# GLA: where VectorE computes the running gate sums and the low parts; mLSTM: where TensorE waits for the meta rows

## The reference, cut to what matters

```python
g = log_sigmoid(a_lr @ w_gla_a2 + b_gla_a) / GLA_TAU      # a log decay for each key feature
def gla_chunk_step(S, xs):
    q, k, v, g = xs
    G = cumsum(g, axis=2)                                  # the running gate sums
    decay = exp(where(causal, G[t] - G[s], -inf))
    A = einsum("bhtk,bhtsk,bhsk->bhts", q, decay, k)
    o = (q * exp(G)) @ S + A @ v
...
o = rms_norm(o, g_gla_head) * silu(r)
y_a = o @ w_br_gla
# mLSTM: q, k (through a convolution), v, and two gates are further columns of the same projection
```

## Time and profile before

| | us |
|---|---|
| median of three executions | 1351.56 |
| lowest and highest of them | 1349.48 and 1355.84 |
| the profiled execution, its own time | 1352.61 |
| its span, first to last instruction | 1350.9 |
| TensorE busy in it | 1294.3 (96%) |
| VectorE busy in it | 622.4 (46%) |
| mean granted TensorE clock | 0.989 of full |

### The profile page before, as it was taken

One profiled execution on the slowest core, in us unless ns is written; L12 is line 12 of the kernel. 1 busy time (PEld: TensorE's weight loads), 2 busy tenths in 40 slices (PEclk: granted clock), 3 DMA queues, 4 the chain that ended last, 5 costly groups with the idle time before them and its releaser, 6 DMA issues.

```text
span 1350.9 us, 17177 instructions
## 1 busy us (share of the span) xinstructions
PE 1294.3 (96%) x6445; PEld 1040.0 (77%) x6448; DVE 622.4 (46%) x1114; ACT 386.8 (29%) x787; POOL 778.0 (58%) x918
## 2 busy tenths in 40 slices
PE   6999889999999999999989999999899999999997
PEld 4866777766898777777888897788678888888886
DVE  3245797773246757462255554232621111333334
ACT  4243334544003333223113344130611111222322
POOL 8367331042663644455765555587467777888882
PEclk9999999999999999999999999999989999999999
DMA  7963200042322212212334332252233333222221
GB/s 179 222 224 90 77 16 16 22 121 60 94 68 61 63 48 63 57 53 64 100 94 112 94 94 81 69 187 94 58 90 94 95 94 115 88 96 96 96 80 63
DMA packets 168441, 121.10 MB, mean 90 GB/s; under 512 B 12264, under 2 KB 146510, under 8 KB 168358
## 3 DMA queue, kind: packets, MB, share of 16 engines
q1 hardware_dynamic: 161654, 108.84, 28.3%
q10 hardware_dynamic: 6704, 11.15, 2.6%
HBM read 115.72 MB, written 9.62 MB: 93 GB/s over the span
## 4 chain that ended last, share of the span: by engine, by line
PE 83%; DVE 9%; DMA 2%; issue 2%; SPq 2%; ACT 1%; POOL 1%; DVEq 0%; ACTq 0%; POOLq 0%
PE GP L1723 40%; PE PA L1758 8%; PE GP L1758 7%; PE GP L1738 6%; PE GP L1720 5%; PE GP L1924 2%; PE PA L1881 2%; DMA wraw<-in_w_in 2%; PE PA L2061 2%; PE PA L1973 1%; PE PA L1904 1%; DVE S L1229 1%; PE PA L1960 1%; DVE top L1228 1%; DVE hres L1648 1%
## 5 line engine op out<-in xcount | busy, mean ns | idle before, releaser
L605 POOL TENSOR_TENSOR wlo<-wraw,whi 128x256 fp32r<-128x256 f32 x712 | 576.6, 840 | 14.9
L601 POOL TENSOR_SCALAR whi<-wraw 128x1024 fp32r<-128x1024 f32 x178 | 194.2, 1091 | 531.0 <-PE GP L1723 261.3
L1723 PE MATMUL GP<-xh,whi 128*128 128x512 f32 x368 | 154.7, 420 | 3.9 <-POOL wlo L605 1.6
L1723 PE MATMUL GP<-xl,whi 128*128 128x512 f32 x368 | 147.4, 400 | 0.0
L1723 PE MATMUL GP<-xh,wlo 128*128 128x512 f32 x368 | 147.1, 400 | 0.0
L1676 DVE TENSOR_TENSOR ul<-U,uh 128x512 fp32r<-128x512 f32 x64 | 65.5, 1060 | 106.6 <-ACT uh L1110 106.6
L1723 PE MATMUL GP<-nh,whi 128*128 128x512 f32 x256 | 102.6, 401 | 0.7 <-DVE nl L1660 0.7
L1723 PE MATMUL GP<-nl,whi 128*128 128x512 f32 x256 | 102.4, 400 | 0.0
L1723 PE MATMUL GP<-nh,wlo 128*128 128x512 f32 x256 | 102.4, 400 | 0.0
L1680 DVE TENSOR_TENSOR U<-U 128x512 f32<-128x512 f32 x32 | 34.5, 1079 | 145.7 <-ACT U L1114 145.7
L1723 PEld LDWEIGHTS GP<-xh,whi 128*128 128x128 f32 x368 | 70.9, 193 | 22.9 <-issue 4.5
(11 more groups left out here) (373 smaller groups left out, 2705.2 us busy)
## 6 DMA issues: line engine op xcount, KB each, us to landing
wraw<-in_w_in SPq DMA_DIRECT2D x75, 512.0 KB, 3.8
wraw<-in_w_up SPq DMA_DIRECT2D x32, 512.0 KB, 4.0
wraw<-in_w_down SPq DMA_DIRECT2D x32, 512.0 KB, 3.6
line_rows<-bias_line SPq DMA_DIRECT2D x1, 5240.0 KB, 26.4
table<-line_rows SPq DMA_DIRECT2D x1, 4096.0 KB, 14.7
wraw<-in_w_br_dsa SPq DMA_DIRECT2D x8, 512.0 KB, 4.1
wraw<-in_w_br_gla SPq DMA_DIRECT2D x8, 512.0 KB, 4.1
wraw<-in_w_br_ml SPq DMA_DIRECT2D x8, 512.0 KB, 4.0
```

What stands on the lines that cost most here:

```text
L601: nc.gpsimd.tensor_scalar(hi, src, 1.0, 1.0, ALU.mult, ALU.mult).then_inc(hi_done, 1)
L605: part = nc.gpsimd.tensor_tensor(lo[:, at:to], src[:, at:to], hi[:, at:to].bitcast(FP32), ALU.subtract)
L1723: ins = mm(ps[0:t.m, 0:SEQ], wt[:, s0, w], av, start=st, stop=sp_)
```

## The change

It has three parts. The function `forget` is cut in two: its PSUM read stays where it was, and the rest becomes `forget_sums`, which VectorE now runs at the off-diagonals, after the second scaling (q = 1); head 0's own is called right after `forget(0)`. `low_parts(0, h - 1)` moves to the off-diagonals too, after the first scaling (q = 0). On TensorE the wait for `xt_ok` moves from ahead of `mq0` to ahead of `mv0M`. No instruction is added or removed, and neither ScalarE's nor GpSimd's order changes.

```diff
--- before.py
+++ after.py
@@ -1336,6 +1336,10 @@
                 g0 = G[:, h % 2, :]
                 dve.wait_ge(gg_l, h + 1)
                 ts(two(g0), halves(ps), cc("a2", h), 0.0, ALU.add, ALU.min).then_inc(gfree[tl[f"gg{h}"].slot], 1)
+
+            def forget_sums(h):
+
+                g0 = G[:, h % 2, :]
                 whole(f"gg{h}")
                 seq(tt(gch[:, :], g0, gch[:, :], ALU.subtract))
                 nc.vector.tensor_tensor_scan(g0[:, 0:META], ones[:, 0:META], gch[:, 0:META], 0.0, ALU.mult, ALU.add)
@@ -1402,6 +1406,10 @@
                     dve.wait_ge(od_ps, 4 * h + q + 1)
                     dve.wait_ge(od_q, 4 * h + q + 1)
                     ts(QQ[:, (j + 1) * P:SEQ], QQ[:, (j + 1) * P:SEQ], gf[:, j + 1:j + 2], None, ALU.mult).then_inc(od_q, 1)
+                    if q == 0 and h:
+                        low_parts(0, h - 1)
+                    if q == 1 and h + 1 < HEADS:
+                        forget_sums(h + 1)
 
             def sum_squares(k):
 
@@ -1445,6 +1453,7 @@
             q_in(0)
             k_in(0)
             forget(0)
+            forget_sums(0)
             for part in range(3):
                 values("gv", 0, part)
             for h in range(HEADS):
@@ -1471,8 +1480,6 @@
                 lv_mul(h, 3)
                 lv_write(h, 4)
                 lv_select(h, 2)
-                if h:
-                    low_parts(0, h - 1)
                 lv_mul(h, 4)
                 lv_write(h, 5)
                 lv_select(h, 3)
@@ -2030,7 +2037,6 @@
             for m in range(KT):
                 gemm(f"ya{m}")
 
-            pe.wait_ge(xt_ok, 2)
             gemm("mq0")
             gemm("mk0")
             pe.wait_ge(u_ok, 1)
@@ -2038,8 +2044,10 @@
             for t in range(QT):
                 nc.tensor.transpose(bank(0)[:, t * HEADS:(t + 1) * HEADS], u[:, t * P:(t + 1) * P], idg)
             nc.tensor.transpose(bank(0)[0:2 * META, QT * HEADS:(QT + 1) * HEADS], um, idg).then_inc(uT_ps, 1)
-            for nm in ("mv0A", "mv0B", "mv0M"):
+            for nm in ("mv0A", "mv0B"):
                 gemm(nm)
+            pe.wait_ge(xt_ok, 2)
+            gemm("mv0M")
             pe.wait_ge(M_ok, 1)
             pe.wait_ge(uT_ok, 2)
 
```

## The result

The changed kernel takes 1341.79 us (median of 4 runs, 1341.07 to 1342.86); the kernel before, run beside it, 1350.91 (4 runs, 1349.48 to 1355.84). The ratio is 0.9925, 95% interval 0.9910 to 0.9941: 0.75% faster. The forecast was 1342.4 in a range of 1338.4 to 1347.5.

A forecast was written before the change was run, and what follows sets the result against it. TensorE, busy 1294.3 of 1350.9 us, was taken to bound the kernel. Gains of 5.8 (level stalls), 1.7 (clock) and 1.7 (mLSTM) make 9.2 us, from the median of 1351.6 to 1342.4, range 1338.4 to 1347.5.

The forecast's parts named there:

- The bound: Whole kernel: TensorE bounds it, so time is won only where TensorE stands still or its clock is low.
- Level stalls, 5.8 us: GLA, ahead of level products 3 and 4: TensorE's stalls of 7.9 us shrink by 5.8 us, ScalarE being late next.
- The moved pieces at nothing: GLA off-diagonals: VectorE's pauses before the second and third scaling hide the moved pieces, at no cost.
- Clock in head 2, 1.7 us: GLA, head 2: with the pause shortened, TensorE's half-clock stretch goes, 1.7 us; head 3's stretch stays.
- mLSTM, 1.7 us: Start of mLSTM: `mv0B` comes 3.4 us earlier, less 1.7 us for a new half-clock stretch inside it.
- the second rival: mLSTM: GpSimd's earlier split of `mq1`'s weight slows VectorE's gate chain, using up the 1.7 us; 1344.1 us, chance 0.15.
- The sum: Whole kernel: level stalls 5.8, clock 1.7 and mLSTM 1.7 give a gain of 9.2 us.
- Slower: Off-diagonals: running sums overrun the pause before the fourth product, with half clock behind; 3.0 us slower, 1354.6 us, chance 0.05.

The follow-up runs named there:

- e6_high_later: Changed kernel with ScalarE's high parts behind the exponential of level 4 in place of ahead of it; 1340.01 us, ratio 0.9917 to the kernel before.
- e3_xt_only: Kernel before with only the wait for `xt_ok` moved from ahead of `mq0` to ahead of `mv0M`; 1349.91 us, ratio 0.9984.
- e7_split_later: Changed kernel with GpSimd waiting for VectorE's gate chain before it splits `mq1`'s weight; 1342.71 us, ratio 0.9938 to the kernel before.
- e12_sums_longer: Changed kernel with eight more scans, which nothing reads, ahead of the running sums in heads 0 to 2; 1350.0 us, ratio 0.9978 to the kernel before.
- e11_values_early: `e8_conv_first` with `e6_high_later`'s order and VectorE's read of `mv0A` ahead of the second convolution; 1337.89 us, ratio 0.9889 to the kernel before.
- e8_conv_first: Changed kernel with the first convolution ahead of VectorE's gate chain and TensorE's transposes behind `mv0A`; 1343.1 us, ratio 0.9933 to the kernel before.

## Why the prediction was right, point by point

- *The bound.* TensorE's idle time and clock account for the difference of the two profiled executions, 11.0 less the 0.24 us lost earlier, against 10.7.
- *Level stalls, 5.8 us.* Measured 6.5. In head 0 all of it went, in heads 1 and 2 2.1 in place of 1.8, in head 3 0.95 in place of 0.7. What is late next is ScalarE with its high parts, as said, and `e6_high_later` confirms it. The term was undersized at the first multiplication: 0.70 us beside the split, where I took 0.94 (the second took 0.96). The rule of the Trainium skill, SBUF — State Buffer, section "SBUF: two separate sides", that the later engine blocks until the other's instruction is over, gives at most 1.24 us each, when the whole of a piece has still to run. The rows, 0.70 and 0.96 us, lie below that, so the most that the rule allows was no price for them, and they do not speak against the rule. The copy of 32 columns in mLSTM, 0.90 us for 0.17, lost 0.73 of the 0.84 that it allows.
- *The moved pieces at nothing.* Right. The idle time before the fourth product stayed at 0.51 us, and the 1.0 us of room that I named is the 1.03 of the trace.
- *Clock in head 2, 1.7 us.* The stretch is gone in both profiles of the changed kernel, 1.6 us, but it was gone as well in `e3_xt_only`, whose head 2 is that of the kernel before to 0.05 us. So the reason that I gave, the shortened pause, is not shown; an edit that leaves the pause alone removes the stretch as well. The stretch of head 3, which I left in the sum, is gone in these two profiles, for another 1.6 us. Over all executions on record the clock gives about 0.8 us in place of the 1.7 of the sum. The Trainium skill, TensorE: Matmul & The Clock Gate, Part 1, says of the slow products at a kernel's start that their number depends on the phase in which the work falls and differs between runs of one kernel. The 9 and 4 of 13 agree with that better than with my count. So do the executions of the kernel before, at 0.986 to 0.992; the two pairs of equal profiles alone would have hidden it.
- *mLSTM, 1.7 us.* Measured 1.3 in the profiled pair, and 1.6 with both orders at full clock. The wait moved to `mv0B` and brought half clock there, as said. But `mv0B` came 2.7 us earlier in relation to `ya7`, not 3.4, and 1.45 us of the wait stood before the transposes, where I had none. The step that failed inside this term is that VectorE's gate chain keeps its length: it took 7.7 us from the logarithm to `uT`, 1.7 more than before, through the split of `mq1`'s weight. That was the second rival's mechanism. It is real (`e7_split_later`), but it costs 0.7 us in the end, since the convolutions get back 1.1 of what the chain loses.
- *The sum.* Two terms missed in opposite directions, stalls by +0.7 and mLSTM by -0.4, and the clock gave 1.5 us more than counted in the profiled executions. The medians differ by 9.1 us, and the ratio makes it 10.1; the 9.2 lies there. That it comes so near is in part luck: with the clock of all executions in place of the profiled pair's, the terms are 6.5, 1.3 and 0.8, 8.6 in all, against 5.8, 1.7 and 1.7 forecast.
- *Slower.* Priced at 1.8 us more idle time in three heads and half clock behind each; `e12_sums_longer` showed 1.67 and two stretches.

## What to carry to other kernels

Price a stall by the distance between two products that should be back to back, and then look for what is late next on a third engine: here 2.0 us of the low parts and 2.1 of the sums bought 6.5 us over four heads because ScalarE came next only 0.4 us behind. A wait that is taken from one product turns up before the next that shares the chain behind it, so follow the chain until a tile is freed early: `e11_values_early` needed the first convolution and then the read of `mv0A` moved. Compare two orders at the same granted clock, in profiles that have no half clock in that place, before calling a difference a gain. A pause in an engine's list is free room of a fixed size: measure it before filling it.

## What the runs showed that I had not expected

- The same 1.56 us pause is followed by half clock in 9 of 13 profiles and by none in 4, and the same 3.15 us pause before `mq0` in two of four, while one of 3.21 us in `e7_split_later` is followed by none. One stretch costs 1.2 to 1.6 us of TensorE's way, and a profile has none to three of them in these stages, up to 0.3% of the time, the size of many an edit.
- Beside GpSimd's split an instruction of VectorE loses an amount that its length does not tell. In the changed kernel the copy of 4 x 32 elements took 0.90 us (0.17 without the split) and the scan of 4 x 528 took 1.68 (1.25): 0.73 and 0.43 lost. In `e8_conv_first` and `e11_values_early` the same two took 0.60 and 1.98: 0.43 and 0.73 lost. The subtraction between them lost 0.36 each time, so the three together lost 1.52 us in each of the three profiles.
